# Retention scores of a hybrid decoder step: turned queries and keys kept as fp16 high and low halves, three fp16 passes in place of an fp32 product

## The chip, the cores and the metric

The kernel runs on one core of one Trainium2 chip, in one launch. The metric is device time in microseconds (us) of that core; lower is better. Engines carry the names that the profile gives them: PE is TensorE (its matmuls), PEld its weight loads, DVE VectorE, ACT ScalarE, POOL GpSimd, SP SyncE, whose only work here is to issue DMAs. PS is PSUM, the memory that PE's matmuls write; the other tiles lie in SBUF.

## The reference, cut to what matters

One layer of a hybrid decoder is computed for a prompt of 1024 rows and for 8 single-row samples: an input LayerNorm, one combined projection, retention and dilated attention side by side, an output projection, a ConvFFN with an added embedding, and two LayerNorms. The change lies in the retention of the prompt, 8 heads of 64 columns in chunks of 128 rows:

```python
def retention_chunk(state, qkv):
    q, k, v = qkv
...
    inner = jnp.einsum('bhij,bjhe->bihe', jnp.einsum('bihd,bjhd->bhij', q, k) * decay, v)
    cross = jnp.einsum('bihd,bhde->bihe', q, state) * jnp.exp(lg[None, :] * (idx[:, None] + 1.0))[None, :, :, None]
    k_dec = k * jnp.exp(lg[None, :] * (C - 1.0 - idx[:, None]))[None, :, :, None]
    new_state = jnp.exp(lg * C)[None, :, None, None] * state + jnp.einsum('bjhd,bjhe->bhde', k_dec, v)
    return new_state, inner + cross
```

The scores are the inner product of q and k over the 64 columns of a head, 128 x 128 for each head and chunk. They are multiplied by a decay mask; q also meets the running state, and k, weighted by its distance from the end of the chunk, updates it.

## The kernel before

The program is a row of stages with a barrier between them: `norm_in`, `retention`, `attention`, `samples`, `mixer`, `ffn`. Only `retention` (lines 343 to 635) is touched. Large products take fp16 operands that are split into a high and a low half, and `PASSES = ((0, 0), (0, 1), (1, 0))` runs high x high, high x low and low x high into one sum. The smaller products of retention have fp32 operands.

Retention works through four pairs of heads, p = 0 to 3. A pair has nine steps s: steps 0 to 7 project one tile of 128 prompt rows each, step 8 the eight sample rows. Every engine runs its own instruction list in order, and in step s each of them also does the later parts of earlier tiles (`tile_at(s, lag, p, kind)` gives the tile that is `lag` steps back; where that falls before step 0, it is a tile of the pair before). After the last pair three more short steps (kind "after") finish what is left over. On PE a step is, in this order:

- L461: 24 fp16 matmuls, the tile's queries, keys, values and gate, 512 columns into one of two PSUM banks (step 8 instead: `product_parts`, 16 matmuls at L99);
- L470, tile s-1: two fp32 transposes of the rotated query and key (`QK`) into `TB`, the first 256 columns of PSUM bank 2;
- L478, tile s-2: the scores, one fp32 product per head with 64 contracted rows, keys as weights and queries as the moving operand, into `SB` (two banks, one per head);
- L490, L492, L494, tile s-3: query times state, masked scores times values, and the update of the state;
- L499, tile s-4: a transpose of the normed and gated output `R` (L502 follows in step 8, and sums the parts of the sample rows).

On DVE a step is: L557, L562, L563 rotate tile s (`turn_pairs`; it begins when the projection of tile s is done); L578 and L579 make `QG` (turned query times powers of the decay) and `KG` (key times its decay) of tile s-1; L585 multiplies the scores of tile s-2 by the decay mask into `SD`; L592 to L603 update the state and take the statistics of tile s-3; L607 makes a low half of tile s-4; L612, in steps 1, 3, 5 and 7, makes the low half of a quarter of the next pair's projection weights; L618 and L622 norm and gate tile s-3 into `R`, after POOL's inverse root (L633). Step 8 ends with the rotation of the sample rows.

ACT copies values and gate out of the projection (L519, L520) and then `TB` into the SBUF tile `QKT` (L526), which is fp32 before, 256 columns for each of two tiles in turn: queries in columns 0 to 127, keys in 128 to 255. From there L478 takes both operands, and L578 the query. PE may write the next transposes into `TB` as soon as this copy is done (`qkt_ready`).

The attention stage (`score`, L851) already forms its scores with three fp16 passes over 64 contracted rows, from a tile that is split in the same way (L948 on ACT, L1021 on DVE).

Of the kernel before, what the change touches and what calls it, by code (L numbers as in the profile page):

```python
# [14 lines left out]
F16 = mybir.dt.float16  # L15
ALU = mybir.AluOpType
ACT = mybir.ActivationFunctionType
# [32 lines left out]
def build(nc, x_prompt, x_sample, cache_k, cache_v, state_ret, state_conv, p_prompt, p_sample,  # L50
# [5 lines left out]
    with outer:  # L56
# [288 lines left out]
        with ExitStack() as st:  # L345
# [3 lines left out]
            QK = sb(st, "QK", [P, 2, 256])  # L349
            QKT = sb(st, "QKT", [P, 2, 256])  # L350
            V = sb(st, "V", [P, NT, P])
# [21 lines left out]
            def UB(t):  # L373
# [3 lines left out]
             out_ready, stats, stats_seen, aggr, var_ready, rstd_ready, state_ready, normed, r_ready, r_turned, rhi,  # L377
             rlo, pe_go, zs_out, w_free, whi, state_zero, z_parts, zp_ready) = sems(
                "z_ready z_turned v_ready halves rotated qkt_ready qg_ready kg_ready scored sd_ready "
                    "out_ready stats stats_seen aggr var_ready rstd_ready state_ready normed r_ready r_turned rhi "  # L380
                    "rlo pe_go zs_out w_free whi state_zero z_parts zp_ready")
            w_in_s = sems("w_in_s0 w_in_s1")
# [30 lines left out]
            with nc.Block() as block:  # L413
# [27 lines left out]
                def _(pe):  # L441
                    def body(pe, p, kind):
                        slot = p % 2
                        for s in range(nsteps(kind)):
# [21 lines left out]
                            if t is not None:  # L466
                                pe.wait_ge(rotated, BASE + 18 * q + 2 * t + 2)
                                pe.wait_ge(qkt_ready, BASE + 8 * q + t)
                                for j in range(2):
                                    mm = nc.tensor.transpose(TB[:, j * P:(j + 1) * P], QK[:, t % 2, j * P:(j + 1) * P], IDENT[:])  # L470
                                mm.then_inc(z_turned, 1)
                            q, t = tile_at(s, 2, p, kind)
                            if t is not None:
                                pe.wait_ge(qkt_ready, BASE + 8 * q + t + 1)
                                pe.wait_ge(sd_ready, BASE + 8 * q + t)
                                for h in range(2):
                                    r = slice(h * E, (h + 1) * E)
                                    mm = nc.tensor.matmul(SB[:, h], QKT[r, t % 2, P:2 * P],  # L478
                                                          QKT[r, t % 2, 0:P], start=True, stop=True)
                                mm.then_inc(scored, 1)  # L480
# [25 lines left out]
                def _(act):  # L506
                    def body(act, p, kind):
                        cols = 384 if kind == "last" else 512
                        for s in range(nsteps(kind)):
# [12 lines left out]
                            if t is not None:  # L522
                                act.wait_ge(z_turned, BASE + 8 * q + t + 1)
                                act.wait_ge(scored, BASE + 8 * q + t - 1)
                                act.wait_ge(qg_ready, BASE + 8 * q + t - 1)
                                nc.scalar.activation(QKT[:, t % 2], TB, ACT.Copy).then_inc(qkt_ready, 1)  # L526
                            q, t = tile_at(s, 4, p, kind)
# [19 lines left out]
                def _(dve):  # L547
# [17 lines left out]
                    def body(dve, p, kind):  # L565
                        cols = 384 if kind == "last" else 512
                        for s in range(nsteps(kind)):
# [6 lines left out]
                            if t is not None:  # L574
                                dve.wait_ge(out_ready, BASE + 8 * q + t - 3)
                                dve.wait_ge(qkt_ready, BASE + 8 * q + t + 1)
                                dve.wait_ge(rotated, BASE + 18 * q + 2 * t + 2)
                                nc.vector.tensor_tensor(QG[:, t % 4], QKT[:, t % 2, 0:P], GQ[:, q, :], ALU.mult).then_inc(qg_ready, 1)  # L578
                                nc.vector.tensor_tensor(KG[:, t % 4], QK[:, t % 2, P:2 * P], KDEC[:, ds(q * P, P)],  # L579
                                                        ALU.mult).then_inc(kg_ready, 1)  # L580
# [1501 lines left out]
```

## Time and profile before

| | |
|---|---|
| Runs of the kernel | median 1517.49 us of 3 (1517.3 to 1518.66) |
| Profiled execution, its own time | 1514.99 us |
| Its span, first to last instruction | 1513.2 us |
| PE busy | 1384.5 us (91% of the span) |
| PEld busy | 785.1 us (52%) |
| DVE busy | 798.9 us (53%) |
| ACT busy | 462.4 us (31%) |
| POOL busy | 273.4 us (18%) |
| Mean granted TensorE clock | 0.978 of full speed |

The span is that of one execution under the hardware profiler, 1.8 us shorter than the execution's own time. Busy shares are of the whole span; what bounds one stage is read from that stage. Ends of matmuls are modelled, so that neighbouring matmuls overlap a little in the rows: the distance between two starts is the better measure of what a group costs on PE. A granted clock of 1.00 is 2.4 GHz, 0.50 is 1.2 GHz.

### The profile page before, as it was taken

What the parts mean: (1) busy time and instruction counts of PE and PEld (TensorE: products, weight loads), DVE (VectorE), ACT (ScalarE), POOL (GpSimd) and SP (SyncE); (2) the same over time, 40 slices, a digit from 0 to 9 for tenths busy, and PEclk for the clock granted to TensorE, in tenths of its full rate; (3) what the DMA queues carried; (4) which work ended last, traced back from release to release, by engine and by line L of the source; (5) the groups of instructions that cost most, each with busy time, mean ns of one, the idle gap of its engine ahead of it and who ended that gap; (6) DMA issues with size and microseconds to landing.
All of it is one profiled execution on the core that took longest, in us unless ns stands there. A gap on an engine that the chain in (4) does not pass through costs nothing. (4 is left out here: it accounts for less than half of the span.)

```text
span 1513.2 us, 23893 instructions
## 1 busy us (share of the span) xinstructions
PE 1384.5 (91%) x8896; PEld 785.1 (52%) x8896; DVE 798.9 (53%) x1601; ACT 462.4 (31%) x753; POOL 273.4 (18%) x329
## 2 busy tenths in 40 slices
PE   2699999979999858999989999999999999999986
PEld 1355555545555433344536664466654666546642
DVE  8566766637667648385524543244431445314457
ACT  3322212227566620041113442034320343202322
POOL 6301010123433306022200110001010010100117
PEclk9999999989999979999999999999999999999998
DMA  7101111027587779350024121022210122101002
GB/s 230 42 29 42 34 38 33 11 66 139 118 158 151 146 171 292 127 173 8 8 58 130 55 82 42 0 62 62 83 42 0 47 77 83 42 0 42 15 14 105
DMA packets 184493, 115.76 MB, mean 76 GB/s; under 512 B 83319, under 2 KB 168263, under 8 KB 184151
## 3 DMA queue, kind: packets, MB, share of 16 engines
q1 hardware_dynamic: 184415, 114.73, 28.8%
q8 instruction: 47, 0.77, 0.2%
q14 instruction: 31, 0.25, 0.1%
HBM read 85.85 MB, written 10.15 MB: 63 GB/s over the span
## 5 line engine op out<-in xcount | busy, mean ns | idle before, releaser
L1731 PE MATMUL PS<-all_HT,all_WS 128*128 128x344 f16 x3168 | 465.4, 310 | 6.6 <-POOLq L73 4.8
L1731 PEld LDWEIGHTS PS<-all_HT,all_WS 128*128 128x128 f16 x3168 | 310.5, 98 | 162.1 <-issue 8.4
L1741 PE MATMUL PS<-all_WS,ffn_HG 128*128 128x512 f16 x608 | 182.4, 379 | 3.6 <-POOL ffn_HG L1891 1.9
L461 PE MATMUL PS<-all_WS,all_HT 128*128 128x512 f16 x768 | 174.9, 386 | 6.1 <-POOLq L73 6.1
L1891 POOL TENSOR_TENSOR ffn_HG<-ffn_PRD,ffn_HG 128x1032 f32 (+1 forms) x22 | 47.2, 2145 | 653.6 <-ACT ffn_HG L1863 653.6
L1851 ACT ACTIVATE ffn_C<-PS,all_CW,all_CWS 128x1032 f32<-128x1032 f32 x44 | 53.0, 1205 | 362.0 <-PE PS L1731 362.0
L818 PE MATMUL PS<-all_WS,all_HT 128*128 128x384 f16 x768 | 132.8, 331 | 3.6 <-POOLq L73 3.6
L461 PEld LDWEIGHTS PS<-all_WS,all_HT 128*128 128x128 f16 x768 | 75.9, 99 | 96.2 <-issue 8.2
L1741 PE MATMUL PS<-ffn_WD,ffn_HG 128*128 128x512 f16 x304 | 115.3, 379 | 0.0
L818 PEld LDWEIGHTS PS<-all_WS,all_HT 128*128 128x128 f16 x768 | 73.5, 99 | 55.0 <-POOLq L73 3.9
L1741 PEld LDWEIGHTS PS<-all_WS,ffn_HG 128*128 (+1 forms) x608 | 59.4, 98 | 76.9 <-issue 6.0
L1948 DVE SCALAR_TENSOR_TENSOR all_HRES<-PS,all_HRES 128x1024 f32 x24 | 29.4, 1225 | 128.9 <-PE PS L1741 128.6
L84 PE MATMUL PS<-all_WS,all_MT 128*128 128x512 f16 x384 | 85.5, 384 | 3.6 <-PEq L709 1.7
L1917 DVE SCALAR_TENSOR_TENSOR all_WS<-ffn_SU,all_WS 128x2048 f16<-128x2048 f32 x21 | 52.0, 2477 | 66.8 <-ACT all_WS L1841 66.8
L1927 DVE TENSOR_SCALAR ffn_UC<-PS 128x10 f32 (+1 forms) x44 | 7.6, 172 | 147.2 <-ACT ffn_CB L1852 147.2
L84 PE MATMUL PS<-mixer_WG,all_HT 128*128 128x512 f16 x384 | 84.2, 379 | 0.0
L633 POOL TENSOR_TENSOR retention_RSTD<-retention_VE,all_EPSC 128x2 f32<-128x2 f32 x32 | 25.4, 794 | 233.8 <-DVE retention_VE L603 233.8
L84 PEld LDWEIGHTS PS<-all_WS,all_MT 128*128 128x128 f16 x384 | 37.5, 99 | 51.0 <-issue 7.2
L888 ACT ACTIVATE attention_PR<-attention_PR,attention_MX 128x128 f32<-128x128 f32 (+7 forms) x64 | 49.1, 767 | 39.6 <-DVE attention_MX L974 39.6
L84 PEld LDWEIGHTS PS<-mixer_WG,all_HT 128*128 128x128 f16 x384 | 37.4, 98 | 43.8 <-issue 0.2
L519 ACT ACTIVATE retention_V<-PS 128x128 f32<-128x128 f32 x32 | 8.9, 277 | 167.6 <-DVE retention_T L557 167.6
L557 DVE TENSOR_TENSOR retention_T<-PS,norm_in_R_ROPE 128x256 f32<-128x256 f32 (+1 forms) x72 | 27.1, 418 | 60.9 <-PE PS L461 47.0
(230 smaller groups left out, 1860.7 us busy)
## 6 DMA issues: line engine op xcount, KB each, us to landing
ffn_SU<-in_w_up SPq DMA_DIRECT2D x42, 512.0 KB, 5.0
ffn_SD<-in_w_down SPq DMA_DIRECT2D x22, 512.0 KB, 3.5
all_STG<-in_w_in SPq DMA_DIRECT2D x32, 256.0 KB, 3.4
all_STG<-in_w_in SPq DMA_DIRECT2D x32, 192.0 KB, 3.3
samples_KC<-in_cache_k_win SPq DMA_DIRECT2D x24, 256.0 KB, 4.6
all_HRES<-in_x_prompt SPq DMA_DIRECT2D x8, 512.0 KB, 8.1
out<-attention_QKV SPq DMA_DIRECT2D x64, 64.0 KB, 1.7
all_STG<-in_w_out SPq DMA_DIRECT2D x8, 512.0 KB, 4.2
```

The source lines that it names most:

```text
L84: mm = nc.tensor.matmul(out[:n], lhs(a, k), w(b, k, c), start=(k == 0 and (a, b) == (0, 0)), stop=(k == kd - 1 and (a, b) == (1, 0)))
L461: mm = nc.tensor.matmul(Z(p, s)[:n], HT[:, a, k, s * P:s * P + n], WS[:, slot, b, k, :], start=(k == 0 and (a, b) == (0, 0)), stop=(k == K ...
L557: nc.vector.tensor_tensor(dst[:n].rearrange("p (g e) -> p g e", e=E // 2), z, ROPE[:n, s, j].unsqueeze(1).broadcast_to([n, 8, E // 2]), AL ...
L633: nc.gpsimd.tensor_tensor(RSTD[:], VE[:], EPSC[:], ALU.pow).then_inc(rstd_ready, 1)
L818: mm = nc.tensor.matmul(Z[:n, g % 2, 0:384], HT[:, a, k, s * P:s * P + n], WS[:, p % 2, b, k, 0:384], start=(k == 0 and (a, b) == (0, 0)), ...
L888: nc.scalar.activation(PR[:, x % 4, 0:w], PR[:, x % 4, 0:w], ACT.Exp, scale=-1.0, bias=MX[:, x % 4:x % 4 + 1], accum_out=SUM[:, x % 4:x % ...
L1731: mm = nc.tensor.matmul(U(x)[:, third], UW[:, u, a, k, x * P:(x + 1) * P], HT[:, b, k, third * T3:(third + 1) * T3], start=(k == 0 and (a, ...
L1741: mm = nc.tensor.matmul(DB[u][:rows, half], HG[:, a, l, ds(t * P, rows)], WD[b][:, l, half * 512:(half + 1) * 512], start=(l == 0 and (a, ...
L1851: nc.scalar.activation(C_from(x, 0), U(x), ACT.Identity, scale=CWS[:, 2, ch], bias=CW[:, 3, ch])
L1891: nc.gpsimd.tensor_tensor(HG[:, 1, l, :], PRD[:], HG[:, 0, l, :], ALU.subtract).then_inc(lo_ready, 1)
L1917: nc.vector.scalar_tensor_tensor(UW[:, u, 1].rearrange("p k n -> p (k n)"), SU[:, u].rearrange("p k n -> p (k n)"), S_W, UW[:, u, 0].rearr ...
L1948: nc.vector.scalar_tensor_tensor(HRES[:n, t], DB[u][:n].rearrange("p b n -> p (b n)"), UNDOWN, HRES[:n, t], ALU.mult, ALU.add).then_inc(ad ...
```

## The change

`QKT` becomes an fp16 tile with two halves for each of its two slots. ACT's copy (L526) now writes the high half. DVE gets one more instruction per tile, which subtracts that half from `TB` and writes the low half (L581 in the changed kernel, announced by a new semaphore `qkt_low`). `QG` is now made from `TB` in PSUM and no longer from `QKT`. The scores run the three passes of `PASSES` with fp16 operands: six matmuls per tile instead of two fp32 ones. Since DVE now reads `TB` too, PE's next transposes also wait for `qkt_low` and `qg_ready` of the tile before.

```diff
-            QKT = sb(st, "QKT", [P, 2, 256])
+            QKT = sb(st, "QKT", [P, 2, 2, 256], F16)
...
                                 pe.wait_ge(qkt_ready, BASE + 8 * q + t)
+                                pe.wait_ge(qkt_low, BASE + 8 * q + t)
+                                pe.wait_ge(qg_ready, BASE + 8 * q + t)
                                 for j in range(2):
                                     mm = nc.tensor.transpose(TB[:, j * P:(j + 1) * P], QK[:, t % 2, j * P:(j + 1) * P], IDENT[:])
...
-                                pe.wait_ge(qkt_ready, BASE + 8 * q + t + 1)
+                                pe.wait_ge(qkt_low, BASE + 8 * q + t + 1)
                                 pe.wait_ge(sd_ready, BASE + 8 * q + t)
-                                for h in range(2):
-                                    r = slice(h * E, (h + 1) * E)
-                                    mm = nc.tensor.matmul(SB[:, h], QKT[r, t % 2, P:2 * P],
-                                                          QKT[r, t % 2, 0:P], start=True, stop=True)
+                                for a, b in PASSES:
+                                    for h in range(2):
+                                        r = slice(h * E, (h + 1) * E)
+                                        mm = nc.tensor.matmul(SB[:, h], QKT[r, t % 2, a, P:2 * P], QKT[r, t % 2, b, 0:P],
+                                                              start=(a, b) == (0, 0), stop=(a, b) == (1, 0))
                                 mm.then_inc(scored, 1)
...
-                                nc.scalar.activation(QKT[:, t % 2], TB, ACT.Copy).then_inc(qkt_ready, 1)
+                                nc.scalar.activation(QKT[:, t % 2, 0], TB, ACT.Copy).then_inc(qkt_ready, 1)
...
                                 dve.wait_ge(qkt_ready, BASE + 8 * q + t + 1)
                                 dve.wait_ge(rotated, BASE + 18 * q + 2 * t + 2)
-                                nc.vector.tensor_tensor(QG[:, t % 4], QKT[:, t % 2, 0:P], GQ[:, q, :], ALU.mult).then_inc(qg_ready, 1)
+                                nc.vector.tensor_tensor(QKT[:, t % 2, 1], TB, QKT[:, t % 2, 0], ALU.subtract).then_inc(qkt_low, 1)
+                                nc.vector.tensor_tensor(QG[:, t % 4], TB[:, 0:P], GQ[:, q, :], ALU.mult).then_inc(qg_ready, 1)
                                 nc.vector.tensor_tensor(KG[:, t % 4], QK[:, t % 2, P:2 * P], KDEC[:, ds(q * P, P)],
                                                         ALU.mult).then_inc(kg_ready, 1)
```

DVE's list at the head of step 7 of the first pair, before:

```order
L557 TENSOR_TENSOR retention_T<-PS,norm_in_R_ROPE 128x256 [waits retention_rotated,retention_z_ready,retention_z_turned]
L557 TENSOR_TENSOR retention_T<-PS,norm_in_R_ROPE 128x256
L562 TENSOR_TENSOR retention_QK<-retention_T 128x4x32 [waits retention_halves]
L563 TENSOR_TENSOR retention_QK<-retention_T 128x4x32
L578 TENSOR_TENSOR retention_QG<-retention_QKT,norm_in_R_GQ 128x128 [waits retention_rotated,retention_qkt_ready,retention_out_ready]
L579 TENSOR_TENSOR retention_KG<-retention_QK,norm_in_R_KDEC 128x128
L585 TENSOR_TENSOR retention_SD<-PS,norm_in_R_DEC 128x256 [waits retention_out_ready,retention_scored]
```

The same place in the changed kernel, whose lines are numbered three or four higher:

```order
L560 TENSOR_TENSOR retention_T<-PS,norm_in_R_ROPE 128x256 [waits retention_rotated,retention_z_ready,retention_z_turned]
L560 TENSOR_TENSOR retention_T<-PS,norm_in_R_ROPE 128x256
L565 TENSOR_TENSOR retention_QK<-retention_T 128x4x32 [waits retention_halves]
L566 TENSOR_TENSOR retention_QK<-retention_T 128x4x32
L581 TENSOR_TENSOR retention_QKT<-PS,retention_QKT 128x256 [waits retention_rotated,retention_qkt_ready,retention_out_ready]
L582 TENSOR_TENSOR retention_QG<-PS,norm_in_R_GQ 128x128
L583 TENSOR_TENSOR retention_KG<-retention_QK,norm_in_R_KDEC 128x128
L589 TENSOR_TENSOR retention_SD<-PS,norm_in_R_DEC 128x256 [waits retention_out_ready,retention_scored]
```

The new L581 stands ahead of `QG` and has taken over its waits, so everything behind it in the step comes one instruction later.

PE's list of step 8 of the first pair, before:

```order
L99 MATMUL PS<-all_WS,all_HTS 16x512 x15
L470 MATMUL PS<-all_IDENT,retention_QK 128x128 [waits retention_qkt_ready,retention_rotated]
L470 MATMUL PS<-all_IDENT,retention_QK 128x128
L478 MATMUL PS<-retention_QKT 128x128 [waits retention_sd_ready,retention_qkt_ready]
L478 MATMUL PS<-retention_QKT 128x128
L490 MATMUL PS<-retention_STATE,retention_QG 128x128 [waits retention_state_ready,retention_kg_ready,retention_normed,retention_qg_ready,retention_sd_ready]
```

And in the changed kernel:

```order
L99 MATMUL PS<-all_WS,all_HTS 16x512 x15
L472 MATMUL PS<-all_IDENT,retention_QK 128x128 [waits retention_qkt_low,retention_qg_ready,retention_qkt_ready,retention_rotated]
L472 MATMUL PS<-all_IDENT,retention_QK 128x128
L481 MATMUL PS<-retention_QKT 128x128 [waits retention_sd_ready,retention_qkt_low]
L481 MATMUL PS<-retention_QKT 128x128 x5
L493 MATMUL PS<-retention_STATE,retention_QG 128x128 [waits retention_state_ready,retention_kg_ready,retention_normed,retention_qg_ready,retention_sd_ready]
```

No instruction of PE changes its place; the scores grow from two to six, and two waits on DVE stand at the transposes.

## Rows read from the trace of the kernel before

**Rows 1.** Retention by engine: stretch, length; PE, PEld, DVE, ACT, POOL busy; clock, DMA, GB/s

```profile
61.00:313.00 252.00, 239.11 (x1319) 128.07 (x1319) 161.08 (x607) 50.28 (x156) 25.41 (x32) 0.99 0.11 33
```

**Rows 2.** Timeline of PE, one inner step: start, us, line, operands, [idle before, releaser]

```profile
99.47 0.38 PE L470 MATMUL PS<-all_IDENT,retention_QK 128*128 128x128 f32 x2
99.78 0.49 PE L478 MATMUL PS<-retention_QKT 64*128 64x128 f32 x4
100.20 0.49 PE L490 MATMUL PS<-retention_STATE,retention_QG 128*128 128x128 f32 x2
...
101.31 5.34 PE L461 MATMUL PS<-all_WS,all_HT 128*128 128x512 f16 x24
106.48 0.38 PE L470 MATMUL PS<-all_IDENT,retention_QK 128*128 128x128 f32 x2
```

**Rows 3.** Who waited for whom on PE, retention stage: total us, times, longest

```profile
PE PS L499 <- DVE retention_R L622: 11.2, 7, 2.7
```

**Rows 4.** Timeline of PE around the ends of pairs 0 and 2 and of the stage

```profile
116.41 0.44 PE L470 MATMUL PS<-all_IDENT,retention_QK 128*128 128x128 f32 x2
...
119.90 0.33 PE L499 MATMUL PS<-all_IDENT,retention_R 128*128 128x128 f32 x1 [1.54 <-DVE retention_R L622]
120.16 1.02 PE L502 MATMUL PS<-retention_ZP,all_SUMS 128*8 128x512 f32 x2
121.11 5.35 PE L461 MATMUL PS<-all_WS,all_HT 128*128 128x512 f16 x24
...
240.00 0.33 PE L499 MATMUL PS<-all_IDENT,retention_R 128*128 128x128 f32 x1 [1.57 <-DVE retention_R L622]
240.26 1.41 PE L502 MATMUL PS<-retention_ZP,all_SUMS 128*8 128x512 f32 x2
241.60 6.61 PE L461 MATMUL PS<-all_WS,all_HT 128*128 128x512 f16 x24
...
313.25 0.47 PE L499 MATMUL PS<-all_IDENT,retention_R 128*128 128x128 f32 x1 [2.72 <-DVE retention_R L622]
317.32 1.14 PE L818 MATMUL PS<-all_WS,all_HT 128*128 128x384 f16 x3 [3.60 <-POOLq L73]
```

**Rows 5.** Timeline of DVE: an inner step, then step 7 of pair 0 to the next pair

```profile
99.72 0.76 DVE L557 TENSOR_TENSOR retention_T<-PS,norm_in_R_ROPE 128x256 f32<-128x256 f32 x2 [1.39 <-PE PS L461]
...
105.51 0.29 DVE L622 TENSOR_TENSOR retention_R<-retention_RN,retention_G 128x128 f32<-128x128 f32 x1
...
113.77 0.76 DVE L557 TENSOR_TENSOR retention_T<-PS,norm_in_R_ROPE 128x256 f32<-128x256 f32 x2 [1.41 <-PE PS L461]
...
115.36 0.29 DVE L578 TENSOR_TENSOR retention_QG<-retention_QKT,norm_in_R_GQ 128x128 f32<-128x128 f32 x1 [0.32 <-issue]
115.57 0.28 DVE L579 TENSOR_TENSOR retention_KG<-retention_QK,norm_in_R_KDEC 128x128 f32<-128x128 f32 x1
115.78 0.42 DVE L585 TENSOR_TENSOR retention_SD<-PS,norm_in_R_DEC 128x256 f32<-128x256 f32 x1
116.11 0.56 DVE L592 SCALAR_TENSOR_TENSOR retention_STATE<-retention_STATE,norm_in_R_GCH,PS 64x64 f32<-64x64 f32 x2
...
126.56 0.75 DVE L557 TENSOR_TENSOR retention_T<-PS,norm_in_R_ROPE 128x256 f32<-128x256 f32 x2 [1.61 <-PE PS L461]
```

**Rows 6.** Timeline of PE, attention's first two scores

```profile
332.19 0.34 PE L851 MATMUL PS<-attention_QKT 64*128 64x128 f16 x6
332.46 4.07 PE L818 MATMUL PS<-all_WS,all_HT 128*128 128x384 f16 x24
...
336.69 0.50 PE L851 MATMUL PS<-attention_QKT 64*128 64x256 f16 x6
337.12 0.66 PE L818 MATMUL PS<-all_WS,all_HT 128*128 128x384 f16 x3
```

**Rows 7.** The low half in attention, one line: duration ns min/median/max, first and last start

```profile
L1021 DVE TENSOR_TENSOR attention_QKT<-PS,attention_QKT x32: 417/424/426, 328.8 to 524.2; 128x256 f16<-128x256 f32 x32
```

**Rows 8.** Granted clock after the end of pair 2, by stretch (columns as in the first group)

```profile
240.60:244.00 3.40, 3.40 (x8) 0.89 (x7) 2.53 (x13) 0.04 (x1) 0.69 (x1) 0.52 0.00 0
```

More of the change, by code:

```diff
@@ L377, in build @@
              out_ready, stats, stats_seen, aggr, var_ready, rstd_ready, state_ready, normed, r_ready, r_turned, rhi,
-             rlo, pe_go, zs_out, w_free, whi, state_zero, z_parts, zp_ready) = sems(
+             rlo, pe_go, zs_out, w_free, whi, state_zero, z_parts, zp_ready, qkt_low) = sems(
                 "z_ready z_turned v_ready halves rotated qkt_ready qg_ready kg_ready scored sd_ready "
                     "out_ready stats stats_seen aggr var_ready rstd_ready state_ready normed r_ready r_turned rhi "
-                    "rlo pe_go zs_out w_free whi state_zero z_parts zp_ready")
+                    "rlo pe_go zs_out w_free whi state_zero z_parts zp_ready qkt_low")
             w_in_s = sems("w_in_s0 w_in_s1")
```

## The prediction

> **What bounds the kernel now.** I first read the stage by engine. In the retention stage PE is busy for 239.1 of 252 us and DVE for 161.1, so PE sets the pace over most of it [rows 1]. The timeline of PE then gives the cost of the scores: from one transpose group to the next a step takes 106.48 - 99.47 = 7.01 us, and the scores (L478) hold PE from 99.78 to 100.20, 0.42 us [rows 2]. The reader is to see there that the groups follow each other without a named wait. Third comes the list of waits, which says where PE does not set the pace: PE waits for DVE's `R` (L622) seven times, 11.2 us in all [rows 3]. Three of these are in step 8 of pairs 0, 1 and 2, 1.54 to 1.57 us each; the other four are in step 8 of pair 3 and behind it, up to 2.72 us [rows 4]. In step 8 PE's projection is short, while DVE still has all of step 7 to do, whose end is `R`. Last I read DVE against PE: in an inner step DVE works from 99.72 to 105.51 + 0.29 = 105.80, 6.08 us, and then idles until PE's next projection is done [rows 5].
>
> So the retention stage has two kinds of stretch. From step 0 of a pair to the end of step 7's projection, PE sets the time. From there to step 8's L499, and from there in pair 3 to the end of the stage, DVE sets it. The change takes time from PE and gives some to DVE, and what each is worth depends on the stretch.
>
> **The change part by part.**
>
> *The scores on PE.* Removed are 32 times two fp32 products, 0.42 us per tile. Added are 32 times six fp16 matmuls of 64 contracted rows and 128 columns. Attention runs exactly this shape in its first score: six matmuls hold PE from 332.19 to 332.46, 0.27 us; with 256 columns they take 337.12 - 336.69 = 0.43, so 0.16 us more for 128 columns more, and a fixed 0.11 [rows 6]. I take 0.27, since operands and shape are the same; that saves 0.15 us per tile. The bounds: at best the fixed 0.11 hides behind the fp32 product that follows, then the group costs 0.16 and saves 0.26. At worst the two heads' matmuls do not run side by side. A projection matmul of 512 columns takes (106.48 - 101.31) / 24 = 0.215 us [rows 2], a quarter of it for 128 columns is 0.054, six are 0.32, with the fixed 0.11 it is 0.43: nothing saved. The Trainium skill (TensorE: Matmul & The Clock Gate, Back-to-back issue gap) speaks against the change more strongly: a stream of weight load and matmul pairs with 128 columns is given as about 81 ns per matmul, an estimate of 0.49 us for six, 0.07 more than the fp32 group; then the change would cost PE time. This trace disagrees with it for this shape: 0.27 / 6 = 45 ns [rows 6].
>
> *How many of the 32 count.* A pair scores its tiles 0 to 6 in steps 2 to 8, and tile 7 in step 0 of the next pair. Steps 2 to 6 of four pairs and step 0 of three are PE's: 20 + 3 = 23. The scores in steps 7 and 8 (two per pair) and the one behind pair 3, nine in all, lie where PE waits for `R` afterwards: what they save only lengthens that wait. So the term is 23 x 0.15 = -3.45 us (bounds 0 and 23 x 0.26 = -5.98).
>
> *The low half on DVE.* Added are 32 subtractions of 128 x 256 from PSUM, written as fp16. Attention's line L1021 is the same instruction: median 424 ns [rows 7]. On DVE the next one starts earlier than that: L585, of the same size and source, starts at 115.78 and its successor at 116.11, 0.33 us later [rows 5]. I take 0.33 on the path; the bounds are 0.21, the distance of the half-sized L578 to L579 (115.36 to 115.57), and the whole 0.42. It can't gain anything, as an instruction that is only added to a list in order. In the PE-bound steps it costs nothing: 6.08 + 0.33 = 6.41 us of DVE stands against 7.01 - 0.15 = 6.86 of PE. If that cover went, each step would grow by the difference. In the DVE-bound stretches it counts in full: once in step 7 of pairs 0, 1 and 2 (3 x 0.33 = +0.99), and twice in pair 3, in step 7 and in step 8, since four of PE's seven waits for `R` follow each other from there to the last L499 at 313.25, behind which the next stage starts at 317.32 [rows 3, 4] (2 x 0.33 = +0.66). Together +1.65 (bounds 5 x 0.21 = +1.05 and 5 x 0.42 = +2.10).
>
> *`QG` from PSUM, ACT's copy as fp16.* Costed at nothing: DVE reads 128 x 128 in either case and starts from the same `qkt_ready`; attention's and retention's neighbours show no dearer form. If it cost 0.1 us, five places would give 0.5, within the range.
>
> *The added waits.* PE's transposes now wait for the tile before's low half and `QG`. In an inner step `QG` starts 115.36 - 113.77 = 1.59 us behind L557, so with the low half ahead of it, it is done at 99.72 + 1.59 + 0.33 + 0.29 = 101.93, some 4.4 us before PE's next transposes at 106.48 - 0.15 [rows 2, 5]. The only close place is step 8, where the transposes come early: `QG` would start at 115.36 + 0.33 = 115.69 and be done at 115.98, and PE arrives at 116.41 less the 0.15 saved in step 7, at 116.26 [rows 4, 5]. That leaves 0.28 us; and if it were used up, the delay would fall into the wait for `R` behind it. Queued behind these waits are L478 to L499 of the step; nobody on DVE is waiting for them there. The scores now wait for `qkt_low` of a tile that DVE finished a whole step earlier. SP and POOL have the same lists as before. The weight halves (L612) come 0.33 us later in step 7, ahead of `R`, for which PE waits anyway.
>
> *Sum.* -3.45 + 0.99 + 0.66 = -1.80 us against the profiled execution's own 1514.99 us, of which its span is 1513.2. That execution lies 2.5 us under the median of the three runs; against the median of 1517.49 it gives **1515.7 us**. About 0.2%, 3.0 us, is what a measurement of this kernel can tell from no change, so the forecast is a small gain that counts as the same.
>
> **The rivals.**
>
> *B: the low half is hidden at the pair ends too.* DVE idles 0.32 us ahead of `QG` [rows 5], and PE might have other work in the wait. Then only the PE term is left: 1517.49 - 3.45 = 1514.0. Against it: the idle 0.32 us ends with ACT's copy, which the low half needs as well, and `R` is what PE's waits end on.
>
> *C: slower, by the clock.* PE's pause ahead of L499 grows from 1.55 us by the 0.33 of DVE and the 0.30 that the scores of steps 7 and 8 save, to about 2.2 us. Before, one such pause of three, the longest by a hair (1.57), was followed by a stretch at a granted clock of 0.52, almost wholly the 1.2 GHz level [rows 4, 8]: there L502 took 1.41 in place of 1.02, and the projection 6.61 in place of 5.35, together 1.65 us lost. If the longer pauses drop the clock after all three pair ends, that is two more: 1517.49 - 1.80 + 3.30 = 1519.0, slower than before. It decides from three on: with two of three the sum is -0.15, with one the forecast holds, with none it is -3.45. For it: a longer pause is what the slow one had. Against it: 1.54 and 1.57 hardly differ, so much of it is chance.
>
> *D: six passes one after the other.* If the two heads' matmuls do not overlap here, the group costs 0.43 and PE saves nothing, while DVE's +1.65 stays: 1519.1. For it: the fp32 products take 0.42 for two heads, with no sign of overlap [rows 2]. Against it: attention's 0.27 for the same six [rows 6]. By the skill's 81 ns, as an estimate, it would be worse by 23 x 0.07 = 1.6, at 1520.7.
>
> **How the numbers follow.** The forecast has 0.60, B 0.15, C 0.13, D 0.12. The forecast's own spread, from the bounds of DVE's share and a pair end more or less in the slow clock, is 1514.0 to 1517.4. The range takes in B and C and stops short of D: **1513.0 to 1519.0 us**; what is left out is D's 0.12 and less than 0.1 of the best bounds. Faster by more than 0.2% means under 1514.46: B nearly whole (0.13) and the part of the forecast in which no pair end falls to the low clock or the fixed 0.11 hides (0.10), so 0.23. Slower by more than 0.2% means over 1520.52, which takes C and D together or the skill's price: 0.04. The same has 0.73.
>
> **What would show it.** Right: the six matmuls (L481) hold PE for about 0.27 us from their start to the next group's, an inner step takes 6.86, the pauses ahead of L502 (L499 before) in step 8 grow from 1.55 to about 2.2, the new L581 lasts 0.42 with its successor 0.33 behind, and DVE's last `R` comes some 1.8 us earlier. Wrong: the six hold PE for over 0.40 (D); pauses in step 8 of 1.9 or less (B); half-clock stretches after all three pair ends (C); or a named wait for `qkt_low` or `qg_ready` at the transposes of inner steps, which nothing in these rows foresees.

## The result, and the profile after

The changed kernel takes 1522.08 us (median of 20 runs, 1517.12 to 1524.91), the kernel before 1518.73 in the same measurement (20 runs, 1517.09 to 1523.52). The ratio is 1.0016, 95% interval 1.0009 to 1.0023: slower by 1.4 to 3.5 us, where 1515.7 was forecast and 1519.0 was the upper end of the range. The profiled execution took 1521.54 us, its span is 1519.7.

The retention stage did what the prediction said. PE's timeline, one inner step of the changed kernel (start, us, line, operands):

```profile
98.76 0.38 PE L472 MATMUL PS<-all_IDENT,retention_QK 128*128 128x128 f32 x2
99.08 0.34 PE L481 MATMUL PS<-retention_QKT 64*128 64x128 f16 x6
99.35 0.49 PE L493 MATMUL PS<-retention_STATE,retention_QG 128*128 128x128 f32 x2
...
105.63 0.38 PE L472 MATMUL PS<-all_IDENT,retention_QK 128*128 128x128 f32 x2
```

The scores hold PE for 99.35 - 99.08 = 0.27 us in place of 0.42 [rows 2], and the step takes 6.87 in place of 7.01. DVE's timeline, where step 7 of pair 0 ends:

```profile
114.36 0.42 DVE L581 TENSOR_TENSOR retention_QKT<-PS,retention_QKT 128x256 f16<-128x256 f32 x1 [0.31 <-PE PS L497]
114.70 0.28 DVE L582 TENSOR_TENSOR retention_QG<-PS,norm_in_R_GQ 128x128 f32<-128x128 f32 x1
...
118.88 0.29 DVE L626 TENSOR_TENSOR retention_R<-retention_RN,retention_G 128x128 f32<-128x128 f32 x1
```

The low half lasts 0.42, and its successor starts 0.34 behind it. PE's timeline around the ends of pairs 0 and 2, which answers to [rows 4]:

```profile
115.26 0.44 PE L472 MATMUL PS<-all_IDENT,retention_QK 128*128 128x128 f32 x2
...
116.25 0.46 PE L493 MATMUL PS<-retention_STATE,retention_QG 128*128 128x128 f32 x2 [0.24 <-DVE retention_STATE L596]
...
119.23 0.33 PE L502 MATMUL PS<-all_IDENT,retention_R 128*128 128x128 f32 x1 [1.85 <-DVE retention_R L626]
119.49 1.02 PE L505 MATMUL PS<-retention_ZP,all_SUMS 128*8 128x512 f32 x2
120.44 7.04 PE L461 MATMUL PS<-all_WS,all_HT 128*128 128x512 f16 x24
...
239.92 0.40 PE L502 MATMUL PS<-all_IDENT,retention_R 128*128 128x128 f32 x1 [1.85 <-DVE retention_R L626]
240.25 1.87 PE L505 MATMUL PS<-retention_ZP,all_SUMS 128*8 128x512 f32 x2
```

Ahead of `R`'s transpose the pause is 1.85 us, and another 0.24 stands ahead of L493: 2.09 in all for 1.55. After pairs 0 and 2 the next work ran at half speed (L461 7.04 for 5.35, L505 1.87 for 1.02), after pair 1 it did not. The table by stretch shows it (length; PE, PEld, DVE, ACT, POOL busy; then the granted clock, DMA share, GB/s), with a stretch in attention as the last row:

```profile
120.60:124.00 3.40, 3.40 (x9) 1.22 (x8) 2.54 (x12) 0.00 (x0) 0.69 (x1) 0.50 0.00 0
181.00:184.40 3.40, 3.40 (x15) 1.29 (x14) 2.53 (x13) 0.04 (x1) 0.69 (x1) 1.00 0.00 0
240.00:243.40 3.40, 3.40 (x7) 0.68 (x8) 2.56 (x13) 0.28 (x1) 0.69 (x1) 0.51 0.00 0
390.20:393.60 3.40, 3.40 (x30) 1.95 (x25) 0.69 (x1) 0.60 (x1) 0.00 (x0) 0.50 0.59 154
```

A clock of 0.50 is the 1.2 GHz level. From its first projection to attention's first matmul the retention takes 316.97 - 61.29 = 255.68 us with two such falls, 256.21 before with one. So the retention is not where the time was lost. What was lost, was lost behind it: from attention's first matmul to the first product of the next stage, samples, that reads the cached values (`samples_VC`, some 63 us into that stage) it takes 307.93 us, before 301.88. Of these 6.05 us, 5.05 lie in attention itself: to the samples' own first matmul it takes 244.16, before 239.11. The first wait that differs there is PE's for the transposed probabilities (the rows name no releaser; in the kernel's text this product waits for the landing of the transposes that SP issues). Before, SP's queue and PE:

```profile
381.65 5.32 SPq L748 DMA_TRANSPOSE attention_PRT<-attention_P  x2
...
389.48 1.53 PE L869 MATMUL PS<-attention_PRT,all_WS 128*64 128x128 f16 x48 [1.83 <-issue]
```

and after:

```profile
381.11 5.90 SPq L752 DMA_TRANSPOSE attention_PRT<-attention_P  x2
...
389.27 1.93 PE L873 MATMUL PS<-attention_PRT,all_WS 128*64 128x128 f16 x48 [2.35 <-issue]
```

Issuing the transposes takes 0.58 us longer, PE waits 0.52 us longer, and the clock falls behind it (the last row by stretch); before it stayed up. The code there is the same: what differs is in the list of DMA queues for just that time. Before (381.65 to 389.40; packets, MB, share of 16 engines):

```profile
q1 hardware_dynamic: 5245, 1.57, 99.9%
```

After (381.1 to 389.2):

```profile
q1 hardware_dynamic: 5248, 1.57, 106.8%
q8 instruction: 1, 0.02, 0.7%
```

One transfer of the instruction queue falls among the transposes. By that queue's records it starts 66.2 us after attention's first matmul; before, the one in its place starts at 60.4, ahead of the transposes. The queue goes with PE's program: from retention to the samples, PE's trace has 244 to 247 matmuls and weight loads between two of its transfers, on average, in each of the 17 profiles taken in all.

It happens a second time, 54 us further on. Before, the transfer starts 114.9 us after attention's first matmul, ahead of the transposes:

```profile
435.47 5.31 SPq L748 DMA_TRANSPOSE attention_PRT<-attention_P  x2
...
443.16 1.53 PE L869 MATMUL PS<-attention_PRT,attention_V 128*64 128x128 f16 x48 [1.48 <-issue]
```

After, it starts at 119.9, together with them:

```profile
436.89 6.45 SPq L752 DMA_TRANSPOSE attention_PRT<-attention_P  x2
...
445.94 2.77 PE L873 MATMUL PS<-attention_PRT,attention_V 128*64 128x128 f16 x48 [3.25 <-issue]
```

### The profile page after: what moved, and what is told of

It is laid out like the page before. It is cut to its first block and busy times, and to the rows that moved or that the text cites. A ratio compares the mean times of both kernels' runs of the same rounds, so it can differ in the third digit from the quotient of the medians.

```text
span 1519.7 us, 24087 instructions
## 1 busy us (share of the span) xinstructions
PE 1389.8 (91%) x8960; PEld 786.4 (52%) x8960; DVE 806.8 (53%) x1633; ACT 462.3 (30%) x753; POOL 273.2 (18%) x329
## 5 line engine op out<-in xcount | busy, mean ns | idle before, releaser
L461 PE MATMUL PS<-all_WS,all_HT 128*128 128x512 f16 x768 | 175.5, 386 | 6.1 <-POOLq L73 6.1
L461 PEld LDWEIGHTS PS<-all_WS,all_HT 128*128 128x128 f16 x768 | 76.1, 100 | 97.1 <-issue 9.6
L1936 DVE SCALAR_TENSOR_TENSOR ffn_C<-PS,all_CWS,ffn_C 128x1032 f32<-128x1032 f32 x44 | 56.8, 1291 | 0.0
```

Of the source, the lines that this page charges most:

```text
L461: mm = nc.tensor.matmul(Z(p, s)[:n], HT[:, a, k, s * P:s * P + n], WS[:, slot, b, k, :], start=(k == 0 and (a, b) == (0, 0)), stop=(k == K ...
L1936: nc.vector.scalar_tensor_tensor(C_from(x, 2), U(x), CWS[:, 0, ch], C_from(x, 2), ALU.mult, ALU.add).then_inc(conved, 1)
```

## The experiments

Theories: **T1**, the clock falls at the pair ends because PE pauses there. **T2**, the longer wait in attention belongs to the program with more PE instructions. **T3**, that wait is chance. Later **TA/TB**: the retention's 2 us do, or do not, reach the kernel's time on equal terms. Ratios are to the kernel before in the same measurement, with 95% intervals; "retention" and "attention" are the two lengths above; a "fall" is a stretch at the 1.2 GHz level behind the end of pair 0, 1 or 2.

**Both kernels again** (no edit).

> The changed kernel itself once more, for a second profile and more times. Two theories. T1 (clock at the pair ends): PE's longer pause ahead of L502 (1.85 us plus 0.24 ahead of L493, where it was 1.54 to 1.57) drops the clock at more pair ends than before, 1.6 us each; then at least two of the three pair ends show a half-clock stretch again, and retention from its first matmul to attention's first lasts 255.7 us or more, where it would be about 252.5 with none. T2 (attention): what was lost lies in attention, in waits for the transposes of the probabilities and half-clock stretches there, which vary by chance from run to run and have nothing to do with the change; then retention comes out 1 to 4 us shorter than the 256.2 of the kernel before, and attention's length differs from the first profile's by some us.

Measured: 1522.67 us, 1.0021 [1.0008, 1.0034]; retention 256.34 with 2 falls, attention 308.54.

> The kernel before, unchanged: a second profile of it. Every time in the stages of the first profile is one draw; four profiles with fp16 scores all took 307.8 to 308.5 us from attention's first matmul to the last stage of samples, the two with fp32 scores 301.9 and 304.6. T1 (clock at pair ends): retention 254.6 plus 1.65 for each pair end at which the clock falls, so 254.6 to 259.5, with no or one fall likelier than three, since the pause ahead of the R transpose is 1.57. T2 (attention's longer waits belong to the program with fp16 scores): attention 301 to 305 again. T3 (they are chance): attention can come out at 307 to 308 here too. Time 1517 to 1520 by the runs already taken.

Measured: 1519.79 us, 0.9998 [0.9988, 1.0007]; retention 259.91 with **3 falls**, attention 303.43. The kernel before falls too, behind pauses of 1.55 to 1.58:

```profile
119.90:123.30 3.40, 3.40 (x7) 0.73 (x6) 2.53 (x13) 0.23 (x1) 0.69 (x1) 0.51 0.00 0
181.40:184.80 3.40, 3.40 (x7) 0.69 (x7) 2.53 (x13) 0.28 (x1) 0.69 (x1) 0.50 0.00 0
242.90:246.30 3.40, 3.40 (x6) 0.70 (x7) 2.56 (x13) 0.28 (x1) 0.69 (x1) 0.50 0.02 5
```

The one fall of the first profile was a lucky draw, not what the kernel usually has.

**The pause filled with unread matmuls.** In fill_after, and with six in fill_before:

```diff
                                 pe.wait_ge(r_ready, BASE + 8 * q + t + 1)
+                                if s == NT:
+                                    pe.wait_ge(rlo, BASE + 8 * q + t)
+                                    for k in range(8):
+                                        nc.tensor.matmul(PS[:, 6], HT[:, 0, k, 0:P], WS[:, slot, 0, k, :], start=True, stop=True)
```

> The changed kernel, with eight matmuls of 512 columns that nobody reads (0.215 us each, 1.72 in all) put into PE's pause ahead of L502 in step 8 of each pair. They fit into the pause of 2.1 us. T1 expects full clock after all three pair ends, retention at 252.5 us, and a time some 3 us under the changed kernel's. T2 expects no or only a small gain in retention and the same time as the changed kernel.

> The kernel before, with six 512-column matmuls into an unread bank in step 8 of each pair, ahead of the R transpose (1.28 us of PE work in a pause of 1.57). T1: no clock fall at a pair end, retention 254.6 (56 us of it untouched), so at most 1.65 us below the first profile's 256.21; the change's own gain with the pauses filled on both sides is then 254.6 - 252.7 = 1.9 us, which is what the prediction's sum said (1.80). Time 1517 to 1518.5. If instead filling helps for a reason that has nothing to do with how long the pause is, the kernel before gains 6 us from it as the changed one did: 1512 to 1513.

Measured: fill_after 1516.28 us, 0.9975 [0.9963, 0.9987], retention 252.68, no fall, attention 307.81. fill_before 1516.97, 0.9979 [0.9970, 0.9988], retention 254.78, no fall, attention 306.97. Pair end 0 of fill_after:

```profile
117.56 1.90 PE L503 MATMUL PS<-all_WS,all_HT 128*128 128x512 f16 x8
119.55 0.33 PE L506 MATMUL PS<-all_IDENT,retention_R 128*128 128x128 f32 x1
119.81 1.02 PE L509 MATMUL PS<-retention_ZP,all_SUMS 128*8 128x512 f32 x2
120.77 5.35 PE L461 MATMUL PS<-all_WS,all_HT 128*128 128x512 f16 x24
```

T1 holds: PE works through the pause, and L461 takes 5.35 again. Both kernels gain from it, so the falls are a cost of both. fill_after gained more than expected: it is 6.4 us under after_again of the same measurement, of which the retention shows 3.7; its second transfer in attention has moved too (below), and the rest was not looked into.

**One part of the change at a time.** nolow is the change without the instruction L581 (the low slots are zero), lowonly the kernel before with that instruction into a tile that nothing reads (PE's next transposes wait for it, as in the change), onepass the change with one of three passes:

```diff
-                                nc.vector.tensor_tensor(QKT[:, t % 2, 1], TB, QKT[:, t % 2, 0], ALU.subtract).then_inc(qkt_low, 1)
```
```diff
+                                nc.vector.tensor_tensor(QKL[:, t % 2], TB, QKT[:, t % 2], ALU.subtract).then_inc(qkt_low, 1)
```
```diff
-                                for a, b in PASSES:
+                                for a, b in PASSES[:1]:
```

> Leaves out the low half of queries and keys: the instruction L581 is gone, the low slot of QKT is set to zero once, and the six matmuls run as in the changed kernel. DVE has as many instructions as before. If my sum is right, each of the five places on DVE's path gets back 0.33 us: retention lasts 252.5 - 1.65 = 250.8 us plus 1.6 for each pair end at half clock, and PE's pause ahead of L502 is 1.8 us. T1 expects fewer half-clock pair ends than in the changed kernel (pause 1.8 in place of 2.1), T2 expects no connection.

> The kernel before with the low half added alone (written to a tile that nobody reads, and awaited by PE's next transposes as in the change); the scores stay fp32 products, QG stays on SBUF. By my sum retention lasts 254.6 + 1.65 = 256.2 us plus 1.6 for each pair end at half clock, with inner steps still at 7.01 and a pause of 1.9 us at the pair ends. T1 expects two or more pair ends at half clock, so about 259.5 and a time some 3 to 5 us above the kernel before; T2 expects about 1.7 us above it.

> The change with the high-times-high pass alone: two score matmuls in place of six, as many PE instructions for the scores as the kernel before had (the two cross passes are left out, the low halves are made and awaited and not read). Scores then hold PE 0.09 to 0.13 in place of 0.27: an inner step is 6.87 - 0.18 = 6.69 where PE bounds it, over 23 steps -3.5 to -4.1, and the pause ahead of the R transpose grows to 1.85 to 2.0, with falls of the clock at two or three pair ends: retention 251.5 to 254. If a step stays at 6.87, PE did not bound it and the scores' saving was never worth its size. T2, in the form that PE's longer program moves what PE waits for in attention: attention back to 301 to 305 here. T3, or T2 by another cause: 307 to 308 again.

Measured: nolow 1518.86 us, 0.9991 [0.9981, 1.0002], retention 253.43 with 2 falls, attention 308.14. lowonly 1522.44, 1.0018 [1.0005, 1.0031], 261.50 with 3, 304.63. onepass 1518.31, 0.9992 [0.9980, 1.0003], 254.75 with 2, 306.26. Two expectations failed. T1 wanted fewer falls in nolow than in the change, and there were two again. T2 wanted attention back at 301 to 305 in onepass, which has 64 matmuls fewer than the kernel before, and it is not: a longer program as such is not the cause. From here on T2 means the place of the instruction transfer. In onepass PE's timeline has

```profile
99.62 0.23 PE L481 MATMUL PS<-retention_QKT 64*128 64x128 f16 x2
99.78 0.49 PE L493 MATMUL PS<-retention_STATE,retention_QG 128*128 128x128 f32 x2
```

so two matmuls hold PE for 0.16 us, more than the 0.09 to 0.13 expected, and the four of the cross passes add 0.11. The step is 6.76, shorter than 6.87 by just that 0.11: PE bounds it, and what the scores save is worth its size there. The pair ends can be read from one length, from step 8's transposes to those of step 1 of the next pair. Without a fall it is 16.69 to 16.70 before, 16.69 in nolow, 17.02 to 17.03 in the change and in onepass; with a fall 1.5 to 1.7 more (18.2 to 18.4 before, 18.6 to 18.7 in the change; two longer falls, in lowonly and onepass, cost 3.0 and 2.8). The low half costs 0.34 there. Behind the last pair, from step 8's transposes to attention's first matmul, the change takes 19.94, nolow 19.28, the kernel before 19.13: the two low halves cost 0.66 there.

**The place of the instruction transfer.** The two kernels again, each with 64 transposes of a corner of the identity into an unread bank, at the end of PE's list of the stage ahead, where PE is idle. They shift all transfers behind them by the same count:

```diff
                             mm.then_inc(par_turned, 1)
+                    for k in range(64):
+                        nc.tensor.transpose(PS[:16, 7, 0:16], IDENT[:16, :16], IDENT[:16, :16])
```

> The change, with 64 transposes of a 16 x 16 corner of the identity into an unread bank, at the end of PE's part of the stage ahead of retention, where PE has nothing else to do for 6 us. They are there for their place in PE's program alone. Attention's wait for transposed probabilities near 72 us was 1.60 to 2.09 us in four profiles with fp32 scores and 2.11 to 2.63 in six with fp16 scores; the records of the instruction queue have a 16 KB transfer 60.0 to 60.4 us after attention's start in the former and 64.0 to 66.2 in the latter, where the transposes of those probabilities (issued at 64.3 to 70 us) run. Kernels with 64 matmuls more and with 64 fewer than before both have it at 65 to 66, so 64 more again should bring it back to 60. T2 (the transfer's place sets the wait): transfer at 60, wait 1.6 to 2.1, attention to samples 302 to 305, time 1517.5 to 1520.5. T3 (the wait has another cause in the change): transfer at 60, wait 2.1 to 2.6, attention 306 to 308.5, time 1521 to 1523.

> The kernel before with the same 64 transposes in the same place. T2: the 16 KB transfer comes at 65 to 66 us after attention's start, the wait near 72 us is 2.1 to 2.6, attention to samples 306 to 308.5, time 1520 to 1523. T3: the wait stays at 1.6 to 2.1 and attention at 302 to 307, time 1518 to 1520.

Measured: **pad_after 1519.12 us, 0.9999 [0.9987, 1.0011]; pad_before 1522.63, 1.0018 [1.0008, 1.0028].** The two kernels have changed places. In pad_after the transfer starts 60.7 us after attention's first matmul, the transposes and PE's wait are those of before, and the DMA list of that time has q1 alone:

```profile
383.49 5.30 SPq L754 DMA_TRANSPOSE attention_PRT<-attention_P  x2
...
391.29 1.53 PE L875 MATMUL PS<-attention_PRT,all_WS 128*64 128x128 f16 x48 [1.75 <-issue]
```

In pad_before it starts at 66.6:

```profile
383.37 6.57 SPq L750 DMA_TRANSPOSE attention_PRT<-attention_P  x2
...
392.07 2.62 PE L871 MATMUL PS<-attention_PRT,all_WS 128*64 128x128 f16 x48 [2.89 <-issue]
```

T3 falls for this wait: it goes with the place of the transfer. The retention takes 258.0 us in both, with three falls each. The length called attention came out at 307.65 in pad_after, where T2 expected 302 to 305, and at 306.96 in pad_before: against T2. In attention itself (to the samples' first matmul) the two part the way T2 says, 239.82 and 241.16; the rest of the length, the opening of the samples, scatters from 62.8 to 69.1 us over the profiles.

Over all 17 profiles the wait follows the transfer. With it at 59.2 to 60.7 us the wait is 1.44 to 2.09 in ten, with it at 64.0 to 66.6 it is 2.11 to 2.89 in seven: no overlap, though the edges touch. The second wait parts more widely: with its transfer 3 us or more ahead of the transposes it is 1.28 to 1.83 in eleven, with the transfer within 0.3 us of their start or among them 2.09 to 3.25 in six. The eleven are the ten and fill_after, whose first transfer is late (64.0, wait 2.63) and whose second is early (116.6, wait 1.74): in one profile, two places and two waits. The length called attention averages 305.2 in the ten and 307.6 in the seven, attention itself 239.4 and 241.5. The pads shift every later transfer and not these two alone, so what the others cost was not separated. Nor are they quite neutral: to retention's first transposes the five padded profiles take 12.1 us on average, the other twelve 12.7.

**The sample sums ahead of `R`'s transpose.** Real work for the pause, with nothing added (reorder is the change so edited, reorder_before the kernel before, pad_reorder the change with the 64 transposes too):

```diff
+                            if s == NT:
+                                pe.wait_ge(zp_ready, BASE + p + 1)
+                                nc.tensor.matmul(Z(p, s)[:NB], SUMS[:], ZP[:], start=True, stop=True).then_inc(z_ready, 1)
                             q, t = tile_at(s, 4, p, kind)
                             if t is not None:
                                 pe.wait_ge(r_ready, BASE + 8 * q + t + 1)
...
-                            if s == NT:
-                                pe.wait_ge(zp_ready, BASE + p + 1)
-                                nc.tensor.matmul(Z(p, s)[:NB], SUMS[:], ZP[:], start=True, stop=True).then_inc(z_ready, 1)
```

> The change, with the product of the sample sums (L505, which holds PE 0.95 us) put ahead of the R transpose in step 8 in place of behind it. Nothing is left out. Its operand has been ready 3 us before. T1: PE's pause ahead of the R transpose falls from 1.85 to 0.8 to 0.9, the clock stays at 2.4 GHz at all four pair ends, and the next pair's first projection starts up to 0.95 us earlier; retention 252.5 without that, and down to 248.7 if each of the four pairs keeps it. Time 1512 to 1516.5. If the clock at the pair ends is not the pause's doing, two of them still fall, and the retention is 255.7 less what the order saves (0 to 3.8): time 1518 to 1522.

> The kernel before with the product of the sample sums put ahead of the R transpose, as in reorder: the change's worth with the pauses short on both sides. T1: pause ahead of the R transpose 0.6 in place of 1.56, no fall of the clock at a pair end, and retention 254.7 less what the order saves there (252.7 to 249.8 was 2.9 in the changed kernel): 251.5 to 252. The change is then worth 2 us in the retention on equal terms; time 1515 to 1517.5, and by the fills (1516.97 against 1516.28) the time shows only 0.7 to 2 of it. If the order gives nothing here, the time is 1516.5 to 1518 and reorder's gain needs the change.

> The change with the sample sums ahead of the R transpose and the 64 transposes of pad_after: both givers-back met at once. T1 and T2: retention 249.8, attention to samples 302 to 305 (307.5 in reorder), time 1510.5 to 1513.5. T1 alone: retention 249.8, attention 306 to 308, time 1514 to 1516.5, as reorder.

Measured: reorder 1515.05 us, 0.9965 [0.9951, 0.9979], retention 249.79. reorder_before 1511.21 in 5 runs, 0.9957 [0.9941, 0.9973], retention 250.95. pad_reorder 1513.7, 0.9962 [0.9950, 0.9974], retention 248.70. No falls. reorder_before came out 3.8 us under the lowest time expected for it, pad_reorder 0.2 over what both theories together gave. Pair end 0 of reorder:

```profile
117.61 1.02 PE L500 MATMUL PS<-retention_ZP,all_SUMS 128*8 128x512 f32 x2
119.53 0.33 PE L505 MATMUL PS<-all_IDENT,retention_R 128*128 128x128 f32 x1 [0.89 <-DVE retention_R L626]
119.69 5.34 PE L461 MATMUL PS<-all_WS,all_HT 128*128 128x512 f16 x24
```

The next projection starts 0.16 us behind `R`'s transpose where it was 1.21. That is 0.3 to 0.4% under the kernel before, with or without the change.

**On equal terms.** The last runs repeat the two orders side by side and put fill_after's transfer where fill_before has it (32 of the transposes).

> The kernel reorder_before again, beside pad_reorder_2: the two have the sample sums ahead of the R transpose and the 16 KB instruction transfer 60 us after attention's start, and differ by the change alone (and by the 64 transposes that place the transfer). The first time it gave 1511.21 us in 5 runs, retention 250.95. Both theories: 1511 to 1513.

> The kernel pad_reorder again. TA (on equal terms the change is worth the 2.1 to 2.3 us that the retention shows, 250.95 against 248.70): 2 us below reorder_before_2, 1509 to 1511. TB (the saving in the retention does not reach the kernel's time): within 0.7 of reorder_before_2, or above it, as the first time (1513.7 in 10 runs against 1511.21 in 5).

> fill_after with 32 of the 16 x 16 transposes at the end of PE's part of the stage ahead: with them PE's program is 128 matmuls longer than before's in all ahead of attention, a whole turn, so the 16 KB transfer comes at 60 us of attention as in fill_before, in place of 64. Wait near 72 us 1.6 to 2.1 (2.63 in fill_after), attention to samples 302 to 307. TA: 2 us below fill_before's 1516.97, 1513.5 to 1515.5; the transfer's place alone takes 1 to 2.8 from fill_after's 1516.28. TB: 1516 to 1517, as fill_after.

Measured: reorder_before_2 1514.7 us, 0.9973 [0.9960, 0.9986], retention 251.20. pad_reorder_2 1513.78, 0.9961 [0.9944, 0.9977], retention 249.00. fill_pad 1514.92, 0.9973 [0.9960, 0.9985], retention 251.74, transfer at 60.3 and wait 1.96 as T2 said. By their times, reorder_before_2 missed its range (1511 to 1513), pad_reorder_2 lies 0.9 us under it and in neither theory's range, fill_pad in TA's. The retention is 2.2 us shorter with the change in both pairs in new order and 3.0 in the filled pair (1.26 of that ahead of the stage's first transposes, 12.03 for 13.29, where the clock rose 2.3 us earlier, ahead of anything that the change touches). The ratios differ by +0.05%, -0.12% and, across two measurements, -0.06%, each with an uncertainty above 0.1% (1.5 us). They fit TA's 2 us (0.13%) only at the edge, and TB as well: **whether the retention's saving reaches the kernel's time in full is left open.**

## Why the prediction was wrong

- *The scores: held.* 0.42 to 0.27 us per tile as read from attention's row; steps of 6.87. Rival D (six passes in series) is out: four matmuls more cost 0.11. The Trainium skill (TensorE: Matmul & The Clock Gate, Back-to-back issue gap) gives about 81 ns per matmul for a stream of weight loads and matmuls of 128 columns. That does not describe this shape here: 0.27 / 6 = 45 ns.
- *The low half: held.* It costs 0.34 at each of three pair ends (forecast 0.33) and 0.66 behind the last pair (forecast 0.66). Rival B (hidden) is out. Its sign did come up by the letter, a pause of 1.85 where 1.9 or less was to speak for B, because another 0.24 of the pause stands ahead of L493, which was not foreseen: PE, quicker by the scores, meets the state update there. It lies in front of the same `R`. `QG` and the added waits at the transposes cost nothing that a row shows.
- *The sum held.* Cut at the transposes, as the rows are, the inner stretches of the pairs are 24 in which a score is saved (one per pair more than the prediction counts, and what it saves comes back behind it): -3.5 us for 24 x -0.15 = -3.60. The three pair ends without a fall give 3 x 0.34 = +1.02 (forecast +0.99), the stretch behind the last pair +0.81 (forecast 0.66 + 0.15 = +0.81). Together **-1.7 for the forecast's -1.80**, falls of the clock apart.
- *The step that failed* is the one that was not written as a term: "-3.45 + 0.99 + 0.66 = -1.80 us against the profiled execution's own" takes all that comes behind the retention as unmoved. The 64 PE matmuls that the change adds were costed as time on PE, and not as length of PE's program. That length moved two instruction transfers, from 60 to 66 and from 115 to 120 us of attention, among the transposes of its probabilities. Price, by the pads: pad_before 1.0018 against the kernel before, 2.7 us [1.2, 4.3]; pad_after against the change, 0.9999 against 1.0016 and 1.0021 in other measurements, 2.6 to 3.3. That is as much as the change lost against the kernel before (1.4 to 3.5).
- *What stays open.* With the transfers in the early place the change differs from the kernel before by -0.2 us [-2.0, +1.7] (pad_after), where the retention's -1.7 alone should stand. The interval just reaches -1.7, and the pairs on equal terms leave it as open. Where that saving goes, if it is lost, no run shows.
- *The base* is a small part of the gap to 1515.7: the three runs shown had a median of 1517.49; further measurements of the same kernel gave 1518.73 to 1520.2.
- *Rival C* had the right price (1.65 us a fall; 1.5 to 1.7 here) and the wrong condition. It took the falls to follow from the longer pause and one in three to be the kernel's habit. With pauses of 1.54 to 1.58 us seven of nine pair ends fell, with 1.84 to 1.85 fourteen of eighteen: the same share. With 0.9 or less, or with the pause filled, none of 24 did. So the change lost nothing here, but neither kernel had its pair ends at full clock, and that is worth more than the change: 3.2 us by fill_before's 0.9979. reorder_before's 0.9973 and 0.9957, 4 to 6.5 us, hold more than the clock: its pair ends take 15.63 to 15.67 us, 1.06 less than the 16.70 of before without a fall.

The block size behind the failed step is on a page: the Trainium skill (Runtime: NRT & Kernel Launch, Instruction fetch mechanics) says that an engine's instructions come in blocks of 16 KiB, 256 instructions, and calls the cost of such a boundary mostly hidden. The profile agrees on the size (page of the profile, after):

```profile
q8 instruction: 48, 0.79, 0.2%
```

0.79 MB / 48 is 16.5 KB. 64 matmuls are 128 records on PE, its loads counted (8960 - 8896 of each kind): half a block. That fits the change and onepass, 64 more and 64 fewer, both at 65 to 66 us. What the runs add is a cost elsewhere than at the boundary: 2.7 us for blocks that came among another queue's transposes.

## What to carry to other kernels

Read a profile of one execution as one draw: before a rival that rests on a clock fall is weighed, see in several profiles how often it falls. An edit that adds instructions to an engine moves its instruction transfers in all that follows; if a stage far from the edit changes, pad both kernels by the same count, so that their transfers change places, before looking for a reason in that stage. And when PE pauses at a regular place, look first for work in its own list that is ready and stands behind the wait: moving one product ahead was worth more than the whole change.

## What was not expected of the hardware

- Where one 16 KB instruction transfer falls among DMA transposes, their issue takes 5.6 to 6.6 us in place of 5.0 to 5.4 (first wait) and 5.5 to 6.5 in place of 4.8 to 5.3 (second), though it moves 1% of the bytes. Why so little does so much was not tried.
- At the first of the two attention waits the clock fell behind each of the eleven of 1.92 to 2.89 us and behind none of the six of 1.44 to 1.83. At the second it fell behind three (2.09, 2.92, 3.25) and stayed up behind 2.18, 2.55 and 2.64. At the pair ends it fell behind most pauses of 1.54 to 1.85. So the length of the pause alone does not decide it; what else does, no run separates.
- Two matmuls of 64 contracted rows and 128 columns, one per head, cost PE 0.055 us as a pair (0.11 for the two cross passes), about what one alone takes by its columns, as an estimate ((106.48 - 101.31) / 24 / 4 = 0.054 [rows 2]): by that the two heads run side by side.
